# Attention B rebuilt: value products one step later, the mask in the bias row, half of the scaling on GpSimd, halved projections between the steps

## What is computed

```python
def swa_mixer(h, w_in, b_in, sinks, w_out, b_out, rel_bias):
    ...
    q, k, v = _split(h @ w_in + b_in, B_SIZES)
    ...
    kk, vv = with_prev(k), with_prev(v)
    logits = jnp.einsum('bnqkgd,bnskd->bnkgqs', q, kk).astype(jnp.float32) * (Dh ** -0.5)
    rel = (W + jnp.arange(W))[:, None] - jnp.arange(2 * W)[None, :]
    in_win = (rel >= 0) & (rel < W)
    ...
    logits = logits + jnp.transpose(bias, (2, 3, 0, 1)).astype(jnp.float32)
    logits = jnp.where(mask[None, :, None, None], logits, -jnp.inf)
    ...
    p = jax.nn.softmax(jnp.concatenate([logits, sink], axis=-1), axis=-1)[..., :-1]
    o = jnp.einsum('bnkgqs,bnskd->bnqkgd', p.astype(vv.dtype), vv)
    return o.reshape(B, T, N_HEADS * Dh) @ w_out + b_out
```

## Time and profile before

| | us |
|---|---|
| median of 3 runs | 1216.76 (1216.35 to 1217.6) |
| the execution with the profile | 1218.91 |
| its span, first to last instruction | 1217.1 |
| PE busy in the span | 1166.9 (96%) |
| DVE, ACT, POOL busy | 594.0, 463.3, 581.3 |
| mean granted clock of PE | 0.989 of 2.4 GHz |

### The profile page before, as it was taken

How to read it: one execution, slowest core, us unless ns; L and a number is a source line. 1 busy time by engine, 2 the same in 40 slices (tenths; PEclk the granted TensorE clock), 3 DMA queues, 4 the chain that set the end, 5 groups by cost and what they waited for, 6 DMA issues and landing times.

```text
span 1217.1 us, 16258 instructions
## 1 busy us (share of the span) xinstructions
PE 1166.9 (96%) x5600; PEld 966.7 (79%) x5600; DVE 594.0 (49%) x1031; ACT 463.3 (38%) x857; POOL 581.3 (48%) x319
## 2 busy tenths in 40 slices
PE   5999999999999999999999989799999999999996
PEld 4767879988888888888888768688888888888885
DVE  5479877746644444432222489846634444321111
ACT  4252347763422233223222467633332223322222
POOL 4344847865444455444444554224444455434441
PEclk9999999999999999999999989899999999999998
DMA  5831411114333323323332542113233332323331
GB/s 167 240 104 35 138 36 53 44 44 127 82 103 103 98 80 97 103 72 95 95 95 61 153 104 53 36 36 103 72 102 103 103 90 83 92 78 93 91 94 69
DMA packets 178468, 110.42 MB, mean 91 GB/s; under 512 B 7180, under 2 KB 173127, under 8 KB 178424
## 3 DMA queue, kind: packets, MB, share of 16 engines
q1 hardware_dynamic: 177984, 108.69, 31.3%
q10 hardware_dynamic: 440, 1.17, 0.3%
HBM read 107.70 MB, written 6.33 MB: 94 GB/s over the span
## 4 chain that ended last, share of the span: by engine, by line
PE 83%; DVE 7%; issue 3%; DMA 2%; POOL 2%; ACT 2%; SPq 0%; ACTq 0%; DVEq 0%; POOLq 0%
PE ps L549 27%; PE ps L551 26%; PE ps L550 26%; POOL w_lo L440 1%; PE ps L755 1%; DMA b_toep<-bias_toep 1%; PE ps L558 1%; DVE work L1430 1%; DMA x_tok<-in_x 1%; DVE ss L1372 1%; DVE b_prob L1672 1%; PE ps L734 1%; DVE xs_lo L1359 1%; DVE work L1414 1%; DMA raw<-in_b_w_in 0%
## 5 line engine op out<-in xcount | busy, mean ns | idle before, releaser
L440 POOL TENSOR_TENSOR w_lo<-raw,w_hi 128x1024 fp32r<-128x1024 f32 (+1 forms) x200 | 463.0, 2337 | 509.7 <-ACT w_hi L973 501.1
L549 PE MATMUL ps<-xs_hi,w_hi 128*128 128x512 f32 (+3 forms) x1024 | 399.7, 390 | 9.1 <-DVE x L1355 3.7
L550 PE MATMUL ps<-xs_lo,w_hi 128*128 128x512 f32 (+3 forms) x1024 | 395.7, 386 | 0.0
L551 PE MATMUL ps<-xs_hi,w_lo 128*128 128x512 f32 (+3 forms) x1024 | 395.5, 386 | 0.0
L973 ACT CAST w_hi<-raw 128x1024 fp32r<-128x1024 f32 (+1 forms) x196 | 178.9, 962 | 435.0 <-PE ps L551 420.4
L549 PEld LDWEIGHTS ps<-xs_hi,w_hi 128*128 128x128 f32 x1024 | 193.1, 189 | 55.1 <-DVE x L1355 4.0
L550 PEld LDWEIGHTS ps<-xs_lo,w_hi 128*128 128x128 f32 x1024 | 193.0, 188 | 39.3 <-issue 1.1
L551 PEld LDWEIGHTS ps<-xs_hi,w_lo 128*128 128x128 f32 x1024 | 193.1, 189 | 38.9
L549 PE MATMUL ps<-act_hi,w_hi 128*128 128x512 f32 x352 | 139.2, 396 | 0.0
L551 PE MATMUL ps<-act_hi,w_lo 128*128 128x512 f32 x352 | 138.0, 392 | 0.0
L550 PE MATMUL ps<-act_lo,w_hi 128*128 128x512 f32 x352 | 136.6, 388 | 0.0
(11 more groups left out here) (186 smaller groups left out, 1389.0 us busy)
## 6 DMA issues: line engine op xcount, KB each, us to landing
raw<-in_ffn_w_gate_up SPq DMA_DIRECT2D x88, 512.0 KB, 4.5
raw<-in_ffn_w_down SPq DMA_DIRECT2D x32, 384.0 KB, 3.6
raw<-in_a_w_in SPq DMA_DIRECT2D x21, 512.0 KB, 4.5
raw<-in_ffn_w_down SPq DMA_DIRECT2D x32, 320.0 KB, 4.0
raw<-in_b_w_in SPq DMA_DIRECT2D x10, 512.0 KB, 5.1
bias_toep<-bias_row SPq DMA_DIRECT2D x1, 4096.0 KB, 22.0
toep<-bias_toep SPq DMA_DIRECT2D x16, 256.0 KB, 2.6
raw<-in_a_w_out SPq DMA_DIRECT2D x8, 512.0 KB, 3.9
```

Source lines behind the costliest of these rows:

```text
L440: nc.gpsimd.tensor_tensor(pieces(w_lo, n)[half], pieces(raw, n)[half], pieces(w_hi, n)[half].bitcast(F32), ALU.subtract)\
L549: nc.tensor.matmul(dst, wh, xh, start=start, stop=False, **kw)
L550: nc.tensor.matmul(dst, wh, xl, start=False, stop=False, **kw)
L551: return nc.tensor.matmul(dst, wl, xh, start=False, stop=stop, **kw)
```

## The change

- The window's mask moves into the bias. The row that the bias is made of grows from 640 to 1024 entries; its second part has the mask in it. SP writes a second skewed copy (`skew_b`) over the first in device memory once attention A has used that, and `b_toep` is loaded from it. POOL's `b_bm` goes, and the minimum reads `b_toep`. The next load waits for the minima instead.
- Sinks are read in place, as columns of `sink` and `nsink`; the copies go.
- The value products of a pair move from the end of step k + 2 to the beginning of step k + 3 (`b_weigh`), so that the loop has eleven steps, 0 to 10. The parts on ACT and DVE follow: the heads come first in a step.
- ACT does the exponents of the first half before it copies the second turned half; DVE does the minima of the first half before the low parts of the second turned half.
- Sums of both halves are added and inverted by one instruction each. The scaling of the first half goes to POOL, that of the second stays on DVE.
- The bias of the queries goes from ACT to POOL.
- Projections: tile 2 comes after the logits of step 0. Tiles 2, 3 (half) in step 0, 3 (half), 4 in step 1, 5 in step 2, half of 6 in step 3, halves of 6 and 7 in step 4, half of 7 in step 5. Tile 3 gets a bank of its own.
- The output projection begins in step 6, in parts of one row block and one tile (`b_out`), for three tiles, and banks change accordingly (`B_OUT_BANK`).
- Slabs 56 to 59 are split at the ends of steps 0, 2, 4 and 7.

```diff
-C_ID, C_DUP, C_CAUSAL, C_WIN, C_HOT = 0, P, 2 * P, 3 * P, 5 * P
-GLEN = 640
+C_ID, C_DUP, C_CAUSAL, C_HOT = 0, P, 2 * P, 3 * P
+ROW_A, ROW_B = 640, 384
+GLEN = ROW_A + ROW_B
...
+FORE, REAR = range(0, DM // 2), range(DM // 2, DM)
+Q_PARTS = {0: ((2, FORE), (2, REAR), (3, FORE)), 1: ((3, REAR), (4, FORE), (4, REAR)), 2: ((5, FORE), (5, REAR)),
+           3: ((6, FORE),), 4: ((6, REAR), (7, FORE)), 5: ((7, REAR),)}
+Q_OF_STEP = {0: (2,), 1: (3, 4), 2: (5,), 4: (6,), 5: (7,)}
+Q_BANK = {0: 2, 1: 3, 2: 4, 3: 5, 4: 4, 5: 4, 6: 4, 7: 4}
+B_OUT_BANK = (4, 1, 2, 3, 0, 1, 2, 3)
+B_SPLITS = {0: S_BQ, 2: S_BQ + 1, 4: S_BQ + 2, 7: S_BQ + 3}
...
-    t[BUCKETS, C_HOT:] = np.where(np.arange(GLEN) >= T, BIG, 0)
+    t[BUCKETS, C_HOT:] = np.where((place >= T) | (np.arange(GLEN) >= ROW_A) & (place < T - P), BIG, 0)
...
+            sp.wait_ge(neg_done, 4 * H)
+            skew_b = bass.AP(tensor=bias_row.tensor, offset=ROW_A + P - 1, ap=[[GLEN, H], [-1, P], [1, 2 * P]])
+            sp.dma_start(bias_toep[:, :, 0:2 * P], skew_b).then_inc(toep_out, 16)
             feed_forward(0, S_F0, S_D0)
...
-                        sp.wait_ge(bbias_done, 2 * (j - 1))
-                    sp.dma_start(b_toep[:, par, a, :], bias_toep[j + a * (H // 2), :, T - 2 * P:T])\
+                        sp.wait_ge(bneg_done, 8 * (j - 1))
+                    sp.dma_start(b_toep[:, par, a, :], bias_toep[j + a * (H // 2), :, 0:2 * P])\
```

More of the change, by code:

```diff
@@ new lines, in b_out @@
+            def b_out(m, ks):
+                n = S_BO + m // 2
+                for k in ks:
+                    pe.wait_ge(bol_done, k + 1)
+                    if k == 0:
+                        pe.wait_ge(lo_done, 2 * n + 2)
+                        pe.wait_ge(*((bqr_done, DM) if m == 0 else (bneg_done, 8 * DM - 6 + 2 * m)))
+                    c = k * 256 + (m % 2) * P
+                    last = mm3(ps[:, B_OUT_BANK[m], :], w_hi[:, n % 2, c:c + P], w_lo[:, n % 2, c:c + P],
+                               bo_hi[:, k, :], bo_lo[:, k, :], k == 0, k == DM - 1)
+                    if k == DM - 1:
+                        last.then_inc(unit_done, 1)
@@ L951, in _ @@
+            for m in range(3):
+                b_out(m, range(6, 7))
+            for m in range(3):
+                b_out(m, range(7, 8))
+            out_rest(S_BO, 3, bo_hi, bo_lo, 3)
             feed_forward(1, 3, S_F1, S_D1)
@@ new lines, in b_exponents @@
+            def b_exponents(k, a):
+                par, j = k % 2, k + a * (H // 2)
+                for i in range(NB):
+                    n = P if i == 0 else 2 * P
+                    at = b_prob[:, par, a, OFFB[i]:OFFB[i] + n]
+                    act.wait_ge(bneg_done, 8 * k + 4 * a + i + 1)
+                    nc.scalar.activation(at, at, ACT.Exp, bias=b_low[:, par, a, i:i + 1], scale=-1.0,
+                                         accum_out=b_rsum[:, par, a, i:i + 1])
+                nc.scalar.activation(b_sinkp[:, par, a, :], b_low[:, par, a, :], ACT.Exp,
+                                     bias=sink[:, j:j + 1]).then_inc(bsinkp_done, 1)
@@ new lines, in b_lowest @@
+            def b_lowest(k, a):
+                par, j = k % 2, k + a * (H // 2)
+                for i in range(NB):
+                    n = P if i == 0 else 2 * P
+                    c0 = (0, P, 0, 2 * P)[i]
+                    dve.wait_ge(blg_done, 4 * k + 2 * (i // 2) + 2)
+                    dve.wait_ge(btoep_full[par], 32 * (k // 2 + 1))
+                    if k >= 2:
+                        dve.wait_ge(bpt_done, 4 * (k - 2) + 2 * a + 2)
+                    nc.vector.tensor_tensor_reduce(
+                        out=b_prob[:, par, a, OFFB[i]:OFFB[i] + n], in0=ps[:, 2 * a + i // 2, c0:c0 + n],
+                        in1=b_toep[:, par, a, 2 * P - n:2 * P], scale=1.0, scalar=nsink[:, j:j + 1],
+                        op0=ALU.add, op1=ALU.min, accum_out=b_low[:, par, a, i:i + 1]).then_inc(bneg_done, 1)
@@ L1683, in _ @@
+            out_proj_b(U_BO, 3, B_OUT)
             feed_forward(1, 3, U_F1, U_D1)
```

290 lines of the change are left out of this document (115 added, 175 removed).

## The result

| | before | changed |
|---|---|---|
| median, us (runs) | 1216.6 (1216.4 to 1217.6; 4) | 1232.5 (1228.8 to 1233.4; 4) |
| ratio | | 1.0119, 95% interval 1.0106 to 1.0133 |
| profiled span, us | 1217.1 | 1231.6 |
| mean granted clock | 0.989 | 0.985 |

A forecast was written before the change was run, and what follows sets the result against it. TensorE (PE), busy nearly throughout, bounds the kernel. New attention B: 0.6 + 97.6 + 17.8 + 1.7 + 2.3 = 120.0 us against 120.5; with the start 0.8 less, 1216.8 - 0.8 = 1216.0 us, range 1208.5 to 1223.

The forecast's parts named there:

- the cost of the skewed copies: Outside attention B: no cost given for the first copy; the second nothing, up to 4 us.
- the walk of the semaphores in attention B: Queues followed forward through attention B's steps: PE's waits sum to 17.8 us, against 15.3 before.
- The second copy: Skewed transfer on SP's queue ahead of the first feed-forward slab: nothing, up to 4 us if as long as the large one.
- The gain of 0.3 us from the smaller table: Constants table shrinks from 640 to 384 columns; PE waits 9.8 us for it; gain 0.3 us (0 to 0.5).
- the small ones of 0.4 and 0.5 in steps 1 and 2: PE's waits in attention B: step 1, 0.4 us for slab 56's low half; step 2, 0.5 us.
- over fifteen: Sign to look for: PE's waits in attention B over fifteen in number, 17 to 18 us in all.
- The hold: Attention B: DVE's sum waits for POOL's low part of the next query, 1.29 us; adds 0.8 to 1.3 a cycle.
- The rival in which DVE goes first: DVE's sum precedes POOL's low part; steps 3 to 6 lose waits of 2.2, 1.2, 1.3, 1.0: 1210.3 us; chance 0.27.
- The clock: Attention B: only the first wait, 3.3 us, brings a half-clock stretch, charged 1.7 us; waits near 2 us charged nothing.
- The rival on the clock: Waits of 1.8 to 2.6 us in steps 3, 4, 5, 6, 8 all bring half-clock stretches: 1222 us; chance 0.22.
- the prediction's point between 1.7 and 2.2 us: Wait length on PE that decides: 1.7 us brought no slow stretch, 2.2 brought 3.4 us at half clock.
- Cheap one-input operations: Rival: POOL's scalings and biases take about half as long as the rows say, 4.2 us less: 1211.8 us; chance 0.06.

The follow-up runs named there:

- two tensors: Changed kernel with the bias rows of the two stages in two HBM tensors, 640 and 384 entries per head: 1222.9 us, 1.0042 of before.
- the order of the start: Third query tile projected before the first logits again, against changed kernel with dense bias rows, second copy in pieces, relaxed tile 4 wait: 1219.3 us (1.0007).
- the scaling: All heads scaled on DVE again, against changed kernel with dense bias rows, second copy in pieces, relaxed tile 4 wait: 1223.9 us (1.0043).
- the place of the move: DVE moves query tile before scaling heads, against changed kernel with dense bias rows, second copy in pieces, relaxed tile 4 wait: 1219.4 us (1.0019).

## Why the prediction was wrong

Two steps of the prediction failed: the cost of the skewed copies, put at nothing, and the walk of the semaphores in attention B, which left out two waits.

**Outside attention B: 8.5 us that I costed at nothing.** "The bias row grows, which DVE copies before a wait for ACT" saw the copy on DVE and not that the rows of 16 heads move from 2560 to 4096 B apart under the first skewed copy. No row of the trace before could size that, and I gave it no upper bound either; it was worth 5.6. The second copy got "nothing, up to 4 us if it takes as long as the large one", because it is half of one that took 22. It took 21.7 and cost 2.9: the bound held, the value taken was wrong, for the bytes were no measure of it. That doubt was the one named as what would make the forecast wrong, and yet no rival had it. The gain of 0.3 us from the smaller table didn't come either: PE waits 10.0 us for it, against 9.8.

**Inside B: two waits left out of the walk.** By steps, predicted and measured: step 0, 3.3 and 3.33; step 3, 2.1 and 1.74; step 4, 1.8 and 1.40; step 5, 1.8 and 1.08; step 6, 2.6 and 2.38; step 7, 1.1 and 0.93; step 8, 1.7 + 2.5 and 1.00 + 2.75. These are good to 0.7 each, their sum was 2.3 too high, and the small ones of 0.4 and 0.5 in steps 1 and 2 didn't come. Missing are 2.54 us in step 1 and 3.82 in step 4, PE's two waits at a projection for DVE's move of the tile before. I followed the values from engine to engine but not `bqr_done`, by which a projection waits for a bank (or, for tile 4, for more than its bank), and DVE does this move last in its step. Predicted 17.8, measured 21.0. The waits are ten, as many as the walk lists; the "over fifteen" of the signs had no working behind it. (In the trace before, the last of the four waits, 0.3, is for DVE as well.) So the sum came within 3.2 us only because terms too high made up for a part of the 6.4 left out.

**The hold: right in three of four steps, and in its order.** The sum lasts 1.93, 1.26 and 1.26 us in steps 3, 4 and 5 of the changed kernel, and in step 4 POOL starts 0.03 us ahead of it; the forecast had 0.05. In step 6 it is short (0.28), against the forecast of over 1; there it is the cast behind POOL's bias, as forecast. The rival in which DVE goes first came true with the bias on ACT in steps 4 and 5. Its price was wrong: 0.2 us for each wait, not 1.2 and 1.3. That the rest of the cycle takes the time back is my reading; no run takes it apart. That version's waits are also shorter than the changed kernel's by 2.4 at the start and by 0.9 in step 6.

**The clock: too low.** After the first wait there are 6.8 us at half clock, not 3.4, and after each of the two waits left out 3.4:

```profile
704.00:710.80 6.80, 5.85 (x31) 5.08 (x32) 3.90 (x18) 4.11 (x17) 2.04 (x2) 0.51 0.14 44
724.60:728.00 3.40, 3.31 (x8) 2.68 (x9) 0.03 (x1) 0.00 (x0) 3.40 (x4) 0.54 1.13 228
765.20:768.80 3.60, 3.53 (x9) 2.82 (x10) 0.01 (x1) 1.30 (x2) 3.49 (x2) 0.53 0.15 46
```

Half of the busy time in them is 6.3 us, against 5.2 in the kernel before and 1.7 forecast. So B grew by 5.7 of waits and 1.1 of clock, less some 0.8 in small gaps. This is one profile: in the twelve others with a first wait of 3.3 us it brought about 3.4 us at half clock, and the wait of 2.54 brought none in five of nine. The rival on the clock priced 1222 from waits near 2 us. None of these brought a stretch in this profile, nor did the one of 2.75; in some of the experiments the one of 2.4 in step 6 did, in some the one of 2.75. So the length of a wait alone doesn't decide, and the prediction's point between 1.7 and 2.2 us is not there.

**Cheap one-input operations** fell: POOL's bias of 128x512 takes 1.57 us and its scaling of 128x256 0.93, as the rows had it, so the rule of the Trainium skill that the prediction quotes (GPSIMD Engine Reference, section 4.1 Engine selection) does not hold here either.

## What to carry to other kernels

When a table in HBM gets wider rows, look at every transfer that reads it: the distance between its rows can set the time, not the bytes, and a power of two is to be tried against values well beside it before it is kept. When a schedule is rewritten, walk the semaphores that give back banks and buffers with the same care as those that hand on values, and ask of each what its engine does before it. An operation moved to an idle engine is not free if it stands ahead of the first work of the bottleneck, or if it starts a few hundredths of a microsecond ahead of another engine's that then waits for its end (0.2 us of PE's time each here).

## What the runs showed that I had not expected

- The skewed copies: 27 us at 4096 B, 22 at 5120, 41 at 8192, with the same rows and bytes.
- Nine profiles have the changed kernel's order of attention B, with the same waits, 20.0 to 21.1 us of them. The stage takes from 123.9 to 127.3 us in them; the difference is the clock. With two tensors the wait of 2.55 us at 713.46 is followed by no slow stretch, where the changed kernel's at 724.68 is:

```profile
713.40:717.00 3.60, 3.54 (x16) 2.93 (x17) 0.01 (x1) 0.00 (x0) 3.54 (x4) 1.00 1.11 221
```

- The same wait of 2.12 to 2.19 us for w_lo, near 120 us in the kernel before and later where the start is late, is followed by a stretch at 1.2 GHz in 8 of the 20 profiled executions and by none in 12. The granted clock is 0.60 in the kernel before and 1.00 in the one with two tensors, in the same window:

```profile
120.00:124.00 4.00, 4.00 (x12) 3.07 (x13) 4.00 (x13) 1.41 (x2) 4.00 (x3) 0.60 0.15 20
```
```profile
120.00:124.00 4.00, 4.00 (x18) 3.31 (x19) 4.00 (x13) 1.34 (x2) 4.00 (x3) 1.00 0.10 12
```

The trace before had shown it once, and I took it as a price that such a wait always has. A single stretch of 3.4 us is worth 1.7, and single executions of one kernel here lie up to 5.8 us apart. So a pair that differs by under 3 us is settled neither by four runs of each nor by one trace of each; that is why the order of the start, the scaling and the place of the move are left open.
